# Index scores of two heads side by side, four buffers of positive parts, four selection rounds of the first tile made early and one of the longest tile made late

## The chip, the cores and the metric

One core of a Trainium2 chip. The metric is the device time of one execution in microseconds (us), lower is better. The kernel before takes 760.4 us (median of 3 runs, 760.36 to 760.41).

Engines are named as the profile names them: PE is TensorE (matrix products), DVE is VectorE, ACT is ScalarE, POOL is GpSimd, SP is SyncE (here the engine that issues most DMAs). PSUM has eight banks of 512 float32 columns.

## What is computed

One layer over 1024 frames of width 1024, batch 1. A projection of the normed input yields the operands of a differential attention (A, 4 heads) and of a sparse attention (B, 8 heads). For B an indexer with 4 heads of width 64 scores every key of every query; each query keeps its 256 best keys:

```
idx_logits = jnp.einsum('bqhd,bkd->bqhk', iqb, ik).astype(jnp.float32)
score = jnp.einsum('bqh,bqhk->bqk', iwb.astype(jnp.float32) * idx_scale,
                   jax.nn.relu(idx_logits))
score = jnp.where(allowed[None], score, -jnp.inf)
_, sel = lax.top_k(score, k_sel)
```

Both branches are gated, joined, projected out, added to x and normed. A frame sees keys up to the end of its own chunk of 64 frames.

## The kernel before

Everything is hand-ordered. Each engine has one instruction list, written out in its own function; engines wait for each other on counting semaphores. Queries go in eight tiles of 128 frames; tile i sees 128*(i+1) keys. Tiles 0 and 1 see at most 256 keys, so only tiles 2 to 7 (`SEL0` = 2) need a selection.

The work comes in this order on PE: turns of x; the indexer's projection in two halves of 512 frames (`project_idx`); the index scores (`score_idx`); the projections of A (`project`, 32 chunks of weights); the attention of A (`attend_all`); the projections of B; the attention of B (`attend_chosen`); the output projection.

**Index scores.** `score_idx(n)` is the product of head n % 4 for tile 2 + n // 4, so n runs from 0 to 23. Even heads lie in the partitions 0 to 63, odd heads in 64 to 127. Each column piece of a score is two matmul records in the trace, since the operands are float32. Scores 0 to 5 are spread over the second half of `project_idx`, one between two blocks of it, since they need only the first half of the keys; the first eight use the banks 1 and 2 in turn, and the later ones four pairs of banks, so that score n waits until the positive part of n-4 (of n-2 for the first eight) has been taken. ACT takes the positive part (`relu_of(n)`) from PSUM into one of two buffers:

```
if n >= 2:
    act.wait_ge(idx_added, n - 1)
act.activation(relu[:, n % 2, 0:length], idx_scores(n, 0, length), ACT.Relu
```

DVE multiplies it by the head's weight and adds it to the tile's score (`add_idx(n)`, L1569 for a tile's first head, L1572 for the others). Around these, ACT and DVE split the turned input for PE into a high and a low part (`high_h`, L788; `low_h`, L1474), and DVE moves the index weights (`move_iwT`, L1546; `move_iw`) and the second half of the keys (`ikT`, L1594), which score 8 is the first to need. The first projection of A starts when the positive part of score 20 has been taken (`idx_relu` 21), and its third, fifth and seventh bank when those of 21, 22 and 23 have.

**Selection.** `select(rounds, first, end)` takes per round and tile the 8 greatest scores (MAX8, L1624) and replaces them by the value `TAKEN` (MATCH_REPLACE8, L1629, with a short MATCH_VALUE_LOAD in front). 256 keys are 32 rounds (for tile 2, which sees 384 keys, the 128 worst are taken off in 16 rounds on the negated scores). All of this is DVE's. 16 rounds of tiles 2 to 7 and one of tiles 6 and 7 lie ahead of the attention of A, the rest of tiles 3 to 7 behind it, during the projections of B. ACT makes a mask of each finished tile (`make_masks`, in `CHOSEN_ORDER`), then moves the last projection of B into `mixB`, which lies on the memory of the scores, and POOL adds masks to bias bands (`near`, L740). The attention of B begins with tile 5 and comes to tile 7 as its seventh.

Of the kernel before, what the change touches and what calls it, by code (L numbers as in the profile page):

```python
# [21 lines left out]
SEQ, D_MODEL = 1024, 1024  # L22
P = 128
# [26 lines left out]
BAND = 2 * P  # L50
SW = 3


# [21 lines left out]
def build(nc, x, norm_w, w_in, w_out, lambda_q1, lambda_k1, lambda_q2, lambda_k2, subln_w,  # L75
# [79 lines left out]
    iwT, _ = place("iwT", [IDX_HEADS, SEQ], f32, at=mask_at)  # L155
    relu, _ = place("relu", [P, 2, SEQ], f32, at=probs_at)
    table, _ = place("table", [BUCKETS, A_HEADS + B_HEADS], f32, at=probs_at)
# [35 lines left out]
    with ctx:  # L193
        def sem(name):
            return ctx.enter_context(nc.semaphore(name))
# [54 lines left out]
        idx_added = sem("idx_added")  # L250
        mask_made = sem("mask_made")
        chosen = sem("chosen")
        mask_bias_made = sem("mask_bias_made")
# [174 lines left out]

        CHOSEN_ORDER = (SEL0, TILES - 2, TILES - 1, *range(SEL0 + 1, TILES - 2))

# [145 lines left out]
        def _(pool):  # L576
# [156 lines left out]
            def near(k):  # L733

                s, m = divmod(near_units[k], 2)
                b, i = place_of(1, s)
                if k >= NEAR:
                    pool.wait_ge(max_ready, 2 * STEPS + near_units[k - NEAR] + 1)
                end = score_off[i] + P * (i + 1)
                pool.tensor_tensor(near_slot(k), bias[:, A_HEADS + 2 * b + m, :], mask[:, end - BAND:end], ALU.add  # L740
                                   ).then_inc(near_made, 1)

            pool.wait_ge(mask_made, TILES - SEL0)
            ahead = [0]
# [27 lines left out]
        def _(act):  # L772
# [64 lines left out]
            def move(g):  # L837
                kind = GROUPS[g][2]
                for t in range(4 if g == Q_GROUP else 0, 8):
# [10 lines left out]
                    else:  # L850
                        if g == B_GROUPS[3] and t == 0:
                            act.wait_ge(mask_made, TILES - SEL0)
                        ins = act.activation((mixA if g == A_GROUPS[3] else mixB)[:, t, :], bank(t),
# [55 lines left out]
            def relu_of(n):  # L909

                length = P * (SEL0 + n // IDX_HEADS + 1)
                act.wait_ge(idx_ready, n + 1)
                if n >= 2:
                    act.wait_ge(idx_added, n - 1)
                act.activation(relu[:, n % 2, 0:length], idx_scores(n, 0, length), ACT.Relu
                               ).then_inc(idx_relu, 1)
# [7 lines left out]
            for n in range(3):  # L924
                relu_of(n)
                high_h(DB + 5 + n)
            high(DB)
            relu_of(3)
            high(DB + 1)
            relu_of(4)  # L930
            high(DB + 2)
            relu_of(5)
            move_iq(1, 0)
# [121 lines left out]
        def _(pe):  # L1055
# [211 lines left out]
            for n in range(3):  # L1267
                score_idx(n)
                project_idx(1, n + 2)
                turn_late(n + 5)  # L1270
            for n in range(3, 6):
                score_idx(n)
                project_idx(1, n + 2)
            score_idx(6)
# [174 lines left out]
        def _(dve):  # L1449
# [109 lines left out]
            def add_idx(n):  # L1559
# [3 lines left out]
                dve.wait_ge(idx_relu, n + 1)  # L1563
                r = relu[:, n % 2, 0:P * (i + 1)]
                if i == SEL0:
# [9 lines left out]
                if h == IDX_HEADS - 1:  # L1575
                    dve.wait_ge(idx_added, n + 1)
                    hidden = score_off[i] if i == SEL0 else score_off[i] + P * (i + 1) - CHUNK
                    link(dve.memset(score[0:CHUNK, hidden:hidden + CHUNK], -UNSEEN if i == SEL0 else UNSEEN))

            move_iwT(0)  # L1580
            low_h(DB + 2)
# [5 lines left out]
            for n in range(3):  # L1587
                add_idx(n)
                low_h(DB + 5 + n)
            for n in range(3, 6):  # L1590
                add_idx(n)
            move_iwT(1)
# [24 lines left out]
            dve.memset(mask_bias[:, 1:2], -MASK_BIAS / 2).then_inc(mask_bias_made, 1)  # L1617

            def select(rounds, first=SEL0, end=TILES, done=()):

                for k in range(rounds):
                    for i in range(first, end):
                        sc = score[:, score_off[i]:score_off[i] + P * (i + 1)]
                        ins = dve.max(top8[:, i - SEL0, :], sc)  # L1624
                        if i == end - 1:
                            link(ins)
                    for i in range(first, end):
                        sc = score[:, score_off[i]:score_off[i] + P * (i + 1)]
                        ins = dve.match_replace(sc, top8[:, i - SEL0, :], sc, TAKEN)  # L1629
                        if k == rounds - 1 and i in done:  # L1630
                            ins.then_inc(chosen, 1)
                        elif i == end - 1:
                            link(ins)

# [92 lines left out]

            select(FIRST, done=(SEL0,))
            select(1, TILES - 2)
            far_min(0, 0, 0)  # L1730
# [21 lines left out]
            link(dve.memset(bias[0:CHUNK, A_HEADS:nh, BAND - CHUNK:BAND], MASKED))  # L1752
            select(ROUNDS - FIRST - 3, SEL0 + 1, done=(TILES - 2, TILES - 1))
            dve.wait_ge(chosen, 3)
            select(1, SEL0 + 1, TILES - 2, done=range(SEL0 + 1, TILES - 2))
            def finishB(s):

# [22 lines left out]

            dve.wait_ge(mask_made, TILES - SEL0)
            far_min(1, 0, 0)
# [85 lines left out]
```

## Time and profile before

| | |
|---|---|
| median of 3 runs | 760.4 us |
| the profiled execution | 760.52 us, of which the span of its instructions 758.6 us |
| PE | 745.5 us busy, 98% |
| DVE | 596.0 us busy, 79% |
| POOL | 348.4 us busy, 46% |
| ACT | 326.3 us busy, 43% |
| granted TensorE clock | 0.999 of full |

The span is the time between the first and the last instruction in the trace; 1.9 us of the execution lie around it. A busy share is an average over stages; the trace has to be read by stage. A row of the timeline has start, length, engine, line, operation, output<-inputs, shape and count; what stands in brackets is how long the engine had been idle before it and who ended that.

### The profile page before, as it was taken

How to read it: one execution, taken by the hardware profiler on the slowest of the kernel's cores; microseconds unless marked ns; L12 is line 12 of the kernel's file. 1: busy time of each engine (PE TensorE's matmuls, PEld its weight loads, DVE VectorE, ACT ScalarE, POOL GpSimd, SP SyncE). 2: the span in 40 equal slices, each digit the busy share in tenths (PEclk: the TensorE clock that was granted, in tenths of full speed). 3: DMA queues.
4: the chain of work that ended last, by engine and by line, in shares of the span. 5: the costliest groups of instructions: out<-in, count | busy, mean ns of one | idle time of the engine just before them, and what ended most of it. 6: DMA issues, size and time to landing. Idle time of an engine off the chain costs nothing.

```text
span 758.6 us, 11943 instructions
## 1 busy us (share of the span) xinstructions
PE 745.5 (98%) x4184; PEld 635.3 (84%) x4184; DVE 596.0 (79%) x1269; ACT 326.3 (43%) x731; POOL 348.4 (46%) x429
## 2 busy tenths in 40 slices
PE   8999999999999999999999999999999999999996
PEld 7756888888888898899888888888999999988886
DVE  5548999999999989888699999996756667435444
ACT  7447122131314666667521221327666666423222
POOL 5220222223556868761334555639999994300000
PEclk9999999999999999999999999999999999999999
DMA  7341111111220010012021111220012022213131
GB/s 275 102 113 54 41 52 47 47 50 46 71 65 1 1 42 20 24 49 79 17 69 55 45 54 43 56 56 28 16 43 57 1 72 71 98 56 106 61 111 57
DMA packets 24564, 44.58 MB, mean 59 GB/s; under 512 B 3076, under 2 KB 10936, under 8 KB 24376
## 3 DMA queue, kind: packets, MB, share of 16 engines
q1 hardware_dynamic: 23352, 42.76, 18.9%
q10 hardware_dynamic: 1152, 1.05, 0.4%
q8 instruction: 34, 0.56, 0.3%
q14 instruction: 26, 0.21, 0.1%
HBM read 35.40 MB, written 6.57 MB: 55 GB/s over the span
## 4 chain that ended last, share of the span: by engine, by line
PE 92%; DVE 3%; issue 2%; ACT 1%; POOL 1%; POOLq 0%; ACTq 0%; DVEq 0%
PE psum L1245 40%; PE psum L1346 12%; PE psum L1443 12%; PE psum L1328 6%; PE psum L1306 4%; PE psum L1309 4%; PE psum L1165 3%; PE psum L1200 3%; PE psum L1137 3%; PE psum L1183 2%; PE psum L1313 1%; PE psum L1361 1%; PE psum L1312 1%; PE psum L1059 1%; DVE probs L1711 1%
## 5 line engine op out<-in xcount | busy, mean ns | idle before, releaser
L597 POOL TENSOR_TENSOR w_lo<-w_raw,w_hi 128x512 fp32r<-128x512 f32 x60 | 77.8, 1299 | 220.0 <-ACT w_hi L781 219.6
L1629 DVE MATCH_REPLACE8 score<-top,score 128x768 f32<-128x768 f32 (+5 forms) x176 | 157.3, 906 | 0.0
L1624 DVE MAX8 top<-score 128x8 f32<-128x768 f32 (+5 forms) x176 | 148.2, 909 | 1.0
L781 ACT ACTIVATE w_hi<-w_raw 128x512 fp32r<-128x512 f32 x60 | 37.6, 630 | 211.9 <-PE psum L1245 208.9
L957 ACT ACTIVATE probs<-psum,small 128x384 f32<-128x384 f32 (+7 forms) x128 | 94.7, 741 | 41.9 <-DVE small L1650 29.8
L1245 PE MATMUL psum<-w_hi,big_hi 128*128 128x512 f32 x256 | 99.6, 389 | 0.0
L1245 PE MATMUL psum<-w_lo,big_hi 128*128 128x512 f32 x256 | 99.6, 389 | 0.0
L1245 PE MATMUL psum<-w_hi,big_lo 128*128 128x512 f32 x256 | 99.6, 389 | 0.0
L1245 PE MATMUL psum<-big_hi,w_hi 128*128 128x512 f32 x192 | 74.8, 390 | 0.0
L1245 PE MATMUL psum<-big_hi,w_lo 128*128 128x512 f32 x192 | 74.7, 389 | 0.0
L1245 PE MATMUL psum<-big_lo,w_hi 128*128 128x512 f32 x192 | 74.7, 389 | 0.0
L1346 PE MATMUL psum<-v,probsT_B 128*128 128x64 f32 x576 | 70.3, 272 | 0.0
L1346 PEld LDWEIGHTS psum<-v,probsT_B 128*128 128x128 f32 x576 | 68.7, 192 | 1.1 <-DVE mixB L1764 0.2
L1328 PE MATMUL psum<-ident,probs 128*128 128x128 f32 x432 | 63.5, 274 | 0.5 <-ACT probsT_B L968 0.3
L1245 PEld LDWEIGHTS psum<-w_hi,big_lo 128*128 128x128 f32 x256 | 48.0, 188 | 10.1
L1245 PEld LDWEIGHTS psum<-w_lo,big_hi 128*128 128x128 f32 x256 | 48.0, 188 | 9.9
L1245 PEld LDWEIGHTS psum<-w_hi,big_hi 128*128 128x128 f32 x256 | 48.0, 188 | 9.9
L1650 DVE TENSOR_REDUCE small<-psum 128x1 f32<-128x384 f32 (+7 forms) x64 | 48.0, 751 | 8.3 <-PE psum L1313 7.5
L1443 PE MATMUL psum<-big_hi,mx_hi 128*128 128x512 f32 (+1 forms) x136 | 51.9, 381 | 0.0
L1328 PEld LDWEIGHTS psum<-ident,probs 128*128 128x128 f32 x432 | 50.3, 147 | 1.6 <-issue 0.5
L1443 PE MATMUL psum<-big_hi,mx_lo 128*128 128x512 f32 (+1 forms) x136 | 51.3, 377 | 0.0
L1443 PE MATMUL psum<-big_lo,mx_hi 128*128 128x512 f32 (+1 forms) x136 | 51.2, 377 | 0.0
(190 smaller groups left out, 1593.8 us busy)
## 6 DMA issues: line engine op xcount, KB each, us to landing
w_raw<-in_w_in SPq DMA_DIRECT2D x62, 256.0 KB, 2.7
xs<-in_x SPq DMA_DIRECT2D x8, 512.0 KB, 7.0
k_high_twice<-k_high_twice SPq DMA_DIRECT2D x16, 256.0 KB, 3.8
xres<-in_x SPq DMA_DIRECT2D x8, 512.0 KB, 4.1
out_y<-y_out SPq DMA_DIRECT2D x8, 384.0 KB, 3.0
w_tail<-in_w_out SPq DMA_DIRECT2D x10, 256.0 KB, 2.9
bias_scratch<-bias_row SPq DMA_DIRECT2D x1, 2304.0 KB
bias<-bias_scratch SPq DMA_DIRECT2D x12, 128.0 KB, 3.1
```

What stands on the lines that cost most here:

```text
L597: pool.tensor_tensor(lo[:, 0:cols], w_staged(n)[:, 0:cols], hi[:, 0:cols].bitcast(f32), ALU.subtract).then_inc(w_lo_made, 1)
L781: act.activation(w_parts(n)[0][:, 0:cols], w_staged(n)[:, 0:cols], ACT.Copy).then_inc(w_hi_made, 1)
L957: act.activation(probs_of(ph, s, m)[:, 0:length], score_of(u, 0, length), ACT.Exp, bias=negmax[:, u % 4:u % 4 + 1], scale=-1.0, accum_out= ...
L1245: ins = pe.matmul(o, a, b, start=(d == 0 and k == 0), stop=(d == DB - 1 and k == 2))
L1306: pe.matmul(o, q[:, qt], k[:, c:c + w], start=True, stop=False)
L1309: ins = pe.matmul(o, q[:, qt], low[:, c:c + w], start=False, stop=not banded)
L1328: ins = pe.transpose(bank(T_BANK + q % 2)[:, k * P:(k + 1) * P], p[:, (j + k) * P:(j + k + 1) * P], ident[:, :])
L1346: ins = pe.matmul(o, probsT[ph][:, q % 4, k * P:(k + 1) * P], v[:, j + k, cols], start=(j + k == 0), stop=(j + k == i))
L1443: ins = pe.matmul(o, a[:, t % 2, e, :], w[:, e, cols], start=(e == 0 and k == 0), stop=(e == DB - 1 and k == 2))
L1624: ins = dve.max(top8[:, i - SEL0, :], sc)
L1629: ins = dve.match_replace(sc, top8[:, i - SEL0, :], sc, TAKEN)
L1650: dve.tensor_reduce(negmax[:, u % 4:u % 4 + 1], score_of(u, 0, P * (i + 1)), AX.X, ALU.min).then_inc(max_ready, 1)
```

## The change

It has four parts.

1. In the second half of the index projection, PE makes the scores of two heads in direct succession (0 and 1, 2 and 3, 4 and 5) behind blocks 2, 3 and 4 of the projection; blocks 5, 6 and 7 follow with no score between them. ACT and DVE follow the same order.
2. The positive parts have four buffers (`RELUS` = 4), so `relu_of(n)` waits for the sum of n-4 where it waited for that of n-2.
3. Four of the sixteen rounds of tile 2 are made as soon as its score is summed (`FIRST_EARLY` = 4), between `low_h` of the last block and the move of the index weights and keys.
4. The one round of tile 7 that lay ahead of the attention of A is made behind all others, at the end of the selection; the mask of tile 7 is made by DVE itself, with a semaphore of its own (`last_mask_made`), for which POOL, ACT and DVE wait only where they need tile 7 or the memory of its score.

```diff
-        CHOSEN_ORDER = (SEL0, TILES - 2, TILES - 1, *range(SEL0 + 1, TILES - 2))
+        CHOSEN_ORDER = (SEL0, TILES - 2, *range(SEL0 + 1, TILES - 2))
...
                         if g == B_GROUPS[3] and t == 0:
-                            act.wait_ge(mask_made, TILES - SEL0)
+                            act.wait_ge(mask_made, len(CHOSEN_ORDER))
+                        if g == B_GROUPS[3] and t == TILES - 2:
+                            act.wait_ge(last_mask_made, 1)
...
-                if n >= 2:
-                    act.wait_ge(idx_added, n - 1)
-                act.activation(relu[:, n % 2, 0:length], idx_scores(n, 0, length), ACT.Relu
+                if n >= RELUS:
+                    act.wait_ge(idx_added, n - RELUS + 1)
+                act.activation(relu[:, n % RELUS, 0:length], idx_scores(n, 0, length), ACT.Relu
...
             for n in range(3):
-                score_idx(n)
+                score_idx(2 * n)
+                score_idx(2 * n + 1)
                 project_idx(1, n + 2)
                 turn_late(n + 5)
-            for n in range(3, 6):
-                score_idx(n)
-                project_idx(1, n + 2)
+            for d in range(5, DB):
+                project_idx(1, d)
...
             for n in range(3):
-                add_idx(n)
+                add_idx(2 * n)
+                add_idx(2 * n + 1)
                 low_h(DB + 5 + n)
-            for n in range(3, 6):
-                add_idx(n)
+            select(FIRST_EARLY, SEL0, SEL0 + 1)
             move_iwT(1)
...
-            select(FIRST, done=(SEL0,))
-            select(1, TILES - 2)
+            select(FIRST - FIRST_EARLY, done=(SEL0,))
+            select(FIRST_EARLY, SEL0 + 1)
+            select(1, TILES - 2, TILES - 1)
...
-            select(ROUNDS - FIRST - 3, SEL0 + 1, done=(TILES - 2, TILES - 1))
-            dve.wait_ge(chosen, 3)
+            select(ROUNDS - FIRST - 3, SEL0 + 1, done=(TILES - 2,))
+            dve.wait_ge(chosen, 2)
             select(1, SEL0 + 1, TILES - 2, done=range(SEL0 + 1, TILES - 2))
+            select(1, TILES - 1)
+            last_score = score[:, score_off[TILES - 1]:score_off[TILES - 1] + SEQ]
+            dve.tensor_scalar(mask[:, score_off[TILES - 1]:score_off[TILES - 1] + SEQ], last_score, TAKEN, MASKED,
+                              ALU.not_equal, ALU.mult).then_inc(last_mask_made, 1)
```

DVE's list from the split of the fifth block of the second half to the move of the keys, before (line 1474 is `low_h`, 1569 and 1572 are `add_idx`, 1546 is `move_iwT`, 1594 the copy of the keys):

```order
L1474 SCALAR_TENSOR_TENSOR big_lo<-psum,nw,big_hi 128x512
L1569 TENSOR_SCALAR score<-relu,iw 128x384
L1474 SCALAR_TENSOR_TENSOR big_lo<-psum,nw,big_hi 128x512
L1572 SCALAR_TENSOR_TENSOR score<-relu,iw,score 128x384
L1578 MEMSET score 64x64
L1569 TENSOR_SCALAR score<-relu,iw 128x512
L1572 SCALAR_TENSOR_TENSOR score<-relu,iw,score 128x512
L1546 TENSOR_SCALAR iwT<-psum 4x512
L1594 COPY ikT<-psum 64x512 x2
```

The same place in the changed kernel, from the sum of score 2 on (line 1478 is `low_h`, 1573 and 1576 `add_idx`, 1589 and 1594 a round of the selection, 1550 and 1614 the moves; of the four early rounds one is shown, and three more like it follow it):

```order
L1576 SCALAR_TENSOR_TENSOR score<-relu,iw,score 128x384 x2
L1582 MEMSET score 64x64
L1478 SCALAR_TENSOR_TENSOR big_lo<-psum,nw,big_hi 128x512
L1573 TENSOR_SCALAR score<-relu,iw 128x512
L1576 SCALAR_TENSOR_TENSOR score<-relu,iw,score 128x512
L1478 SCALAR_TENSOR_TENSOR big_lo<-psum,nw,big_hi 128x512
L1589 MAX top_71<-score 128x8
L1594 MATCH_REPLACE score<-top_71,score 128x384
...
L1550 TENSOR_SCALAR iwT<-psum 4x512
L1614 COPY ikT<-psum 64x512 x2
```

The sums now lie ahead of the last split, and the rounds stand where the sums of scores 3 to 5 stood, ahead of the move of weights and keys.

The end of the selection on DVE in the changed kernel (line 1763 makes the mask of tile 7; the row before the first one here is the last round of tiles 3 to 7; ISA at 1659 is the first step of the attention of B, `far_min`, which before followed directly on the row with 128x768):

```order
L1589 MAX top_71<-score 128x8 x3
L1594 MATCH_REPLACE score<-top_71,score 128x512
L1594 MATCH_REPLACE score<-top_71,score 128x640
L1594 MATCH_REPLACE score<-top_71,score 128x768
L1589 MAX top_71<-score 128x8
L1594 MATCH_REPLACE score<-top_71,score 128x1024
L1763 TENSOR_SCALAR mask<-score 128x1024
L1659 ISA psum,small<-psum,mask 128x512
```

A round of tile 7 and one more instruction now lie between the last round of tiles 3 to 5 and the attention of B.

## Rows read from the trace of the kernel before

**Rows 1.** The page, its first part: busy time, share, instructions.

```profile
PE 745.5 (98%) x4184; PEld 635.3 (84%) x4184; DVE 596.0 (79%) x1269; ACT 326.3 (43%) x731; POOL 348.4 (46%) x429
```

**Rows 2.** Busy us by stretch: length, PE, PEld, DVE, ACT, POOL; granted clock; DMA.

```profile
34.20:54.40 20.20, 20.20 (x79) 12.04 (x78) 7.79 (x12) 7.95 (x14) 4.12 (x3) 1.00 0.44 118
54.40:71.60 17.20, 16.65 (x73) 9.12 (x72) 14.73 (x22) 12.58 (x18) 0.00 (x0) 1.00 0.25 76
71.60:246.70 175.10, 175.10 (x775) 145.11 (x775) 172.25 (x309) 43.77 (x71) 61.92 (x55) 1.00 0.16 46
```

**Rows 3.** PE's timeline from 34 to 72 us, around the index scores (L1165).

```profile
34.20 0.91 PE L1165 MATMUL psum<-ikT,iqT 64*128 64x384 f32 x2
35.03 0.45 PE L1137 MATMUL psum<-big_hi,widx_hi 128*68 128x512 f32 x1
...
47.84 1.12 PE L1165 MATMUL psum<-ikT,iqT 64*128 64x512 f32 x2
48.89 0.45 PE L1137 MATMUL psum<-big_hi,widx_hi 128*68 128x512 f32 x1
...
54.41 1.13 PE L1165 MATMUL psum<-ikT,iqT 64*128 64x512 f32 x4
...
56.23 1.83 PE L1165 MATMUL psum<-ikT,iqT 64*128 64x512 f32 x8 [0.34 <-ACT relu L915]
...
71.63 0.50 PE L1245 MATMUL psum<-big_hi,w_hi 128*128 128x512 f32 x1
```

**Rows 4.** ACT's timeline: positive parts of scores 6 and 7, and of 19.

```profile
55.58 1.08 ACT L915 ACTIVATE relu<-psum 128x512 f32<-128x512 f32 x2 [0.46 <-PE psum L1165]
...
68.75 0.92 ACT L915 ACTIVATE relu<-psum 128x896 f32<-128x896 f32 x1 [0.37 <-DVE score L1572]
```

**Rows 5.** DVE's timeline from 45 to 71 us.

```profile
45.59 0.75 DVE L1474 SCALAR_TENSOR_TENSOR big_lo<-psum,nw,big_hi 128x512 fp32r<-128x512 f32 x1 [2.24 <-ACT big_hi L788]
46.49 1.38 DVE L1572 SCALAR_TENSOR_TENSOR score<-relu,iw,score 128x384 f32<-128x384 f32 x1
...
53.70 0.68 DVE L1546 TENSOR_SCALAR iwT<-psum 4x512 f32<-4x512 f32 x1
54.42 1.40 DVE L1594 COPY ikT<-psum 64x512 f32<-64x512 f32 x2
...
63.19 3.26 DVE L1572 SCALAR_TENSOR_TENSOR score<-relu,iw,score 128x768 f32<-128x768 f32 x3
...
67.50 3.66 DVE L1572 SCALAR_TENSOR_TENSOR score<-relu,iw,score 128x896 f32<-128x896 f32 x3
```

**Rows 6.** POOL's timeline at the end of the index projection.

```profile
46.16 2.83 POOL L597 TENSOR_TENSOR w_lo<-w_raw,w_hi 128x512 fp32r<-128x512 f32 x2 [21.60 <-ACT w_hi L781]
```

**Rows 7.** Groups of DVE by shape, the selection: busy us, mean ns of one.

```profile
L1624 DVE MAX8 top<-score 128x8 f32<-128x1024 f32 x32 | 38.7, 1209 | 0.0
...
L1629 DVE MATCH_VALUE_LOAD score<-top,score 128x8 f32 x176 | 14.6, 83 | 1.1
...
L1624 DVE MAX8 top<-score 128x8 f32<-128x384 f32 x16 | 9.0, 560 | 0.5
L1629 DVE MATCH_REPLACE8 score<-top,score 128x384 f32<-128x384 f32 x16 | 8.7, 543 | 0.0
```

**Rows 8.** DVE's timeline where the attention of A begins.

```profile
246.70 1.07 DVE L1650 TENSOR_REDUCE small<-psum 128x1 f32<-128x384 f32 x2 [0.72 <-PE psum L1313]
```

**Rows 9.** Timelines before B's attention (DVE, ACT, POOL), and a 1024-wide TENSOR_SCALAR.

```profile
526.18 0.70 DVE L1655 CUSTOM_DVE_ANT_0 psum<-psum,mask 128x512 f32<-128x512 f32 x1 [5.98 <-PE psum L1309]
...
521.26 4.69 ACT L853 ACTIVATE mixB<-psum 128x512 f32<-128x512 f32 x8
...
527.55 0.90 ACT L957 ACTIVATE probs<-psum,small 128x768 f32<-128x768 f32 x1 [0.30 <-DVE small L1678]
...
521.32 2.57 POOL L740 TENSOR_TENSOR near_low<-bias,mask 128x256 f32<-128x256 f32 x4 [0.50 <-ACT mask L874]
...
71.38 0.75 DVE L1569 TENSOR_SCALAR score<-relu,iw 128x1024 f32<-128x1024 f32 x1
```

More of the change, by code:

```diff
@@ L51 @@
 SW = 3
+RELUS = 4
+FIRST_EARLY = 4
 def bucket_selector():
@@ L155, in build @@
     iwT, _ = place("iwT", [IDX_HEADS, SEQ], f32, at=mask_at)
-    relu, _ = place("relu", [P, 2, SEQ], f32, at=probs_at)
+    relu, _ = place("relu", [P, RELUS, SEQ], f32, at=probs_at)
     table, _ = place("table", [BUCKETS, A_HEADS + B_HEADS], f32, at=probs_at)
@@ L251, in build @@
         mask_made = sem("mask_made")
+        last_mask_made = sem("last_mask_made")
         chosen = sem("chosen")
@@ L736, in near @@
                 b, i = place_of(1, s)
+                if i == TILES - 1:
+                    pool.wait_ge(last_mask_made, 1)
                 if k >= NEAR:
@@ L741, in near @@
                                    ).then_inc(near_made, 1)
-            pool.wait_ge(mask_made, TILES - SEL0)
+            pool.wait_ge(mask_made, len(CHOSEN_ORDER))
             ahead = [0]
@@ L924, in _ @@
             for n in range(3):
-                relu_of(n)
+                relu_of(2 * n)
+                relu_of(2 * n + 1)
                 high_h(DB + 5 + n)
[L927 to L932, printed above, removed]
+            for n in range(DB, DB + SW):
+                high(n)
             move_iq(1, 0)
@@ L1563, in add_idx @@
                 dve.wait_ge(idx_relu, n + 1)
-                r = relu[:, n % 2, 0:P * (i + 1)]
+                r = relu[:, n % RELUS, 0:P * (i + 1)]
                 if i == SEL0:
@@ L1578, in add_idx, with select @@
                     link(dve.memset(score[0:CHUNK, hidden:hidden + CHUNK], -UNSEEN if i == SEL0 else UNSEEN))
+            def select(rounds, first=SEL0, end=TILES, done=()):
+                for k in range(rounds):
+                    for i in range(first, end):
+                        sc = score[:, score_off[i]:score_off[i] + P * (i + 1)]
+                        ins = dve.max(top8[:, i - SEL0, :], sc)
+                        if i == end - 1:
+                            link(ins)
+                    for i in range(first, end):
+                        sc = score[:, score_off[i]:score_off[i] + P * (i + 1)]
+                        ins = dve.match_replace(sc, top8[:, i - SEL0, :], sc, TAKEN)
+                        if k == rounds - 1 and i in done:
+                            ins.then_inc(chosen, 1)
+                        elif i == end - 1:
+                            link(ins)
             move_iwT(0)
@@ L1617, in _ @@
             dve.memset(mask_bias[:, 1:2], -MASK_BIAS / 2).then_inc(mask_bias_made, 1)
[L1619 to L1633, printed above, removed]
             def later(ins):
@@ L1779, in mix_low @@
                                       ).then_inc(mixT_lo, 1)
-            dve.wait_ge(mask_made, TILES - SEL0)
+            dve.wait_ge(mask_made, len(CHOSEN_ORDER))
+            dve.wait_ge(last_mask_made, 1)
             far_min(1, 0, 0)
```

## The prediction, made before the changed kernel ran

> **What bounds the kernel now.** I read the page first: PE is busy 745.5 of 758.6 us [rows 1], so work that PE stops doing, or waits that it stops making, are what can be won, and the other engines matter only where PE waits for them. Next I read busy time by stretch [rows 2]. While the second half of the index projection runs (34.2 to 54.4 us), PE is busy all of its 20.2 us, DVE 7.8 and ACT 8.0: PE is the bound and the others have room. From 54.4 to 71.6 us DVE is busy 14.7 of 17.2 us, ACT 12.6, while PE's weight loads take 9.1: this stretch is a chain between three engines. Then come 175 us of projections in which PE is busy all the time and so is DVE, with the selection. The granted clock is 1.00 in all of these (2.4 GHz), so no part of the sum hangs on the clock.
>
> Third, PE's timeline [rows 3]. One score alone, 384 keys wide, holds PE from 34.20 to 35.03 us; one of 512 keys from 47.84 to 48.89. At 54.41 scores 6 and 7 stand together: four matmul records in 1.13 us, where two records took 1.12. So a second head, on the other half of the partitions, costs nothing when it directly follows the first. This row is of the kernel before; only scores 0 to 5 stand apart there.
>
> Last, the two places where DVE's selection meets PE. At the start of the attention of A, DVE waited 0.72 us for PE [rows 8]: DVE was on time by less than a microsecond. At the start of the attention of B it waited 5.98 us [rows 9], so its selection ended at 520.20.
>
> **Part 1, the pairs.** PE loses three slots: those of scores 1 and 3 (384 wide, 35.03 - 34.20 = 0.83 each) and one of the 512-wide pair 4 and 5 (48.89 - 47.84 = 1.05) [rows 3]. That is 2.7 us. Three entries from the projection's full array into the half array go too; I can't read their price from one row, and take 0 to 0.3 us for them. Score 1 now waits earlier for the move of the band and the index weights on DVE; those precede the split whose wait on ACT leaves DVE over 2 us idle, and lie before 34.2 us. Nothing else on PE waits: the splits that blocks 5 to 7 need are done one block ahead, behind two positive parts and two sums instead of one, in a stretch where ACT and DVE are idle over half of the time [rows 2].
>
> The Trainium skill (TensorEngine Tiling (Array Packing), Key Properties) says that tiles operate independently but that a change of the tiling mode drains TensorE; by the first half three slots go, as the rows say, and by the second somewhat more than their length goes, which is the 0 to 0.3 us above.
>
> **Part 3, the early rounds, and what they put off.** They stand ahead of the move of the keys, which score 8 needs. The last split began at 45.59 us [rows 5]; in the new order it comes 0.2 us later (block 4 now follows a 512-wide pair, 1.05, and not a 384-wide score, 0.83), so DVE comes free at about 46.5. A round of 384 is 0.56 + 0.54 us and a value load of 0.08 [rows 7]; each of the two steps waits for the one before, and I add 0.03 to 0.04 us for each of these: 1.24 us, four make 5.0 us, to 51.5. Then the index weights and keys: 0.72 us to the start of the copies and 1.40 for them [rows 5] bring 53.6 us. Without the rounds score 8 would start where PE and ACT allow: at 56.23 before [rows 3], right behind the first positive part of the pair 6 and 7 (55.58 and some 0.6, half of 1.08 and an overlap [rows 4]), less 2.7 to 3.0, that is 53.2 to 53.5. The rounds thus hold score 8 back by 0.1 to 0.4 us, whatever part 1 gives above 2.6. I take **2.6 us** for parts 1 and 3 together at this point, 2.2 to 2.9 as bounds. The sums of 6 and 7 and all that follow move by the same.
>
> **Part 2, four buffers.** From 60 us on DVE sums without a gap, so DVE's own times don't move against score 8; what moves is who waits for it. Before, the positive part of score 19 waited for the sum of 17, the first of the three sums at 67.50 that make 3.66 us; with a step of 1.25 us it ends at 68.65, and the part starts at 68.75 (0.37 us idle, ended by DVE) and takes 0.92 [rows 4, 5]. Score 23 needs its bank, starts at 69.7 and ends in 1.8 to 1.9 us, and at 71.63 A's projections begin [rows 3]. With four buffers the same part waits for the sum of 15, the last of three that start at 63.19 and take 3.26: 66.45 us. That is 68.65 - 66.45 = **2.2 us** earlier, if ACT and PE are ready then. I stepped through them with the durations of the trace and the waits of the changed list, and it is close: ACT ends the part of 18 at about 66.5, and PE by itself, with pairs of 1.3 to 1.7 us, could be done by 68.5 against the 69.4 that this step asks for. So the three engines are nearly equal, and I keep 1.4 as the low bound and 2.3 as the high. The parts of 21, 22 and 23 end in time for the third, fifth and seventh bank: the last one waits for the sum of 19, at 67.50 + 3.66 = 71.16, and ends at 72.2, while PE, begun at 69.4, comes to the seventh bank 4.1 us later at 73.5.
>
> The Trainium skill (TensorEngine Tiling (Array Packing), PSUM Bottleneck) says that tiling speeds up TensorE but not the emptying of PSUM, which may then bind. By it the pairs could not pay where ACT and DVE bind; here they don't in the stretch of part 1, and part 2 acts on just that bound in the next.
>
> **At the attention of A.** PE comes 2.6 + 2.2 = 4.8 us earlier. DVE comes earlier by 2.6, by four rounds of tile 2 in the interleaved list (some 1.0 each, 4.0) and by a round of tile 7 (about 2.3, from 1.21 for each step [rows 7] less overlap): 8.9 us. Its 0.72 us of waiting [rows 8] becomes 4.8. Without parts 3 and 4 it would be 2.6 + 0.72 = 3.3 against 4.8, and PE would wait 1.5 us: that is what the moved rounds bring, and the cover that the sum needs.
>
> **At the attention of B, part 4.** All is shifted by 4.8 us; I keep the old times. After 520.20 us DVE makes one round of 1024: 1.21 + 0.08 + 1.21 [rows 7] and the joints, 2.6. Then the mask of tile 7, which no row shows: at least 0.75 us (a TENSOR_SCALAR of the same width [rows 9]), at most the 1.21 of the other passes over 1024. I take 0.9, since it is nearest to the first. It ends at 523.7, 2.4 us before DVE's first work there (526.18). ACT reaches the bank that waits for it at 521.26 + 6 x 0.59 = 524.8 [rows 9], 1.1 us later still than the mask. POOL needs tile 7 much later. Price: nothing.
>
> **Sum.** 2.6 + 2.2 = 4.8 us. The profiled execution took 760.52 us, 1.9 around its span of 758.6, 0.1 from the median; its span becomes 753.8 and the median 760.4 - 4.8 = **755.6 us**. What follows each of the shifted points (attention, output projection) has the same order as before.
>
> **The rivals.**
>
> *The pairs alone (chance 0.10).* ACT or PE bind in the index scores, and the four buffers bring less than 1 us. For it: the three engines are within a microsecond there. Against it: ACT was idle for DVE ahead of the part of 19, and the next bound, PE's, is 0.9 us away. Time 760.4 - 2.6 - 0.5 = 757.3.
>
> *The mask of tile 7 comes late (0.06).* The seven bands that POOL makes from 521.32 us on (0.64 each, to 525.8 [rows 9]) would stretch or stop DVE's mask step. For it: at 46.49 a sum of 384 took 1.38 us beside POOL's work at 46.16 [rows 5, 6], where sums of 768 take 1.09. If the mask waited for the last band, it would be made at 526.6; ACT's last two banks would end at 527.8 and not 525.95, and the first exponential, at 527.55 with 0.30 us to spare, would come 1.5 us late: 755.6 + 1.5 = 757.1. Against it: by the 768-wide sums a 384-wide one takes at most 0.7 us, so POOL cost that sum 0.7 to 0.8; put here, these leave the mask before 524.8. The Trainium skill (GPSIMD Engine Reference, Specifications table) says that GpSimd's interfaces to SBUF are shared with VectorE and contended for by instructions with two SBUF inputs or in a two-port mode; the sum above is of the first kind and the trace agrees, and the mask step could be of the second.
>
> *Slower (0.03).* The early rounds hold the keys back for much longer than 5 us. For a loss of 1.5 us they would have to put score 8 off by some 6.5 us more, a round of 2.8 us and not 1.24. It is decided at 2.4 us a round (no change). Against it: 16 such rounds are in the trace, at 0.56 and 0.54. Time about 762.
>
> *No change (0.03).* PE wins its 4.8 us and waits for them at one of the two attentions. It takes a DVE that is 9 us later at A, or 7 at B, than worked out above.
>
> **How the numbers follow.** The forecast has 0.78; its own range is 2.2 + 1.4 = 3.6 to 2.9 + 2.3 = 5.2 us won, 755.2 to 756.8. The range reaches on to the first two rivals and a little to the fast side, for startup waits that I hold fixed: 754.7 to 757.4. What can be told from no change is 0.2%, 1.5 us: faster 0.94, same 0.03, slower 0.03.
>
> **What would show it.** In the changed profile: four records of scores at each of about 34.2, 37.7 and 41.3 us, in no more time than two took; scores 6 and 7 at 51.4 to 51.7; score 8 at 53.6, behind the copy of the keys; the part of 19 no longer idle for more than 0.1 us for DVE; the first projection of A at 66.8; DVE idle 4 to 5 us at the start of A's attention near 242, and 2 to 3 us at B's. It would be wrong if the first projection came after 68, or PE had a new wait of a microsecond at either attention.

## The result, and the profile after

The changed kernel takes 755.55 us (median of 4 runs, 754.80 to 757.23) against 760.40 us; the ratio is 0.9939, with a 95% interval of 0.9926 to 0.9951. (Here and below the ratio is taken over all executions, so it is not exactly that of the two medians.) A second set of runs of the changed kernel took 755.68 us (5 runs, 754.96 to 757.45). The profiled execution took 755.46 us, its span is 753.7 us, where 753.8 was forecast.

Busy time in the stretches that answer to [rows 2], of the changed kernel (us, then PE, PEld, DVE, ACT, POOL, granted clock, DMA):

```profile
34.20:51.40 17.20, 17.20 (x80) 11.45 (x80) 11.20 (x24) 7.89 (x15) 3.81 (x3) 1.00 0.48 139
51.40:66.80 15.40, 13.80 (x73) 8.48 (x70) 13.52 (x20) 12.25 (x17) 0.00 (x0) 1.00 0.29 85
66.80:241.90 175.10, 175.10 (x775) 145.18 (x776) 167.91 (x297) 43.45 (x71) 61.96 (x56) 1.00 0.17 46
```

The first stretch is 3.0 us shorter and the second 1.8; the third is as long as before, and DVE has 7 us free in it where it had 3.

PE's timeline of the changed kernel, answering to [rows 3]; L1169 is `score_idx`, L1249 the first projection of A:

```profile
34.00 0.92 PE L1169 MATMUL psum<-ikT,iqT 64*128 64x384 f32 x4
37.53 0.92 PE L1169 MATMUL psum<-ikT,iqT 64*128 64x384 f32 x4
41.06 1.13 PE L1169 MATMUL psum<-ikT,iqT 64*128 64x512 f32 x4
...
51.06 1.13 PE L1169 MATMUL psum<-ikT,iqT 64*128 64x512 f32 x4
...
53.54 1.36 PE L1169 MATMUL psum<-ikT,iqT 64*128 64x512 f32 x8 [1.02 <-DVE ikT L1614]
55.48 11.24 PE L1169 MATMUL psum<-ikT,iqT 64*128 64x512 f32 x56 [0.58 <-DVE iw L1560]
66.66 0.50 PE L1249 MATMUL psum<-big_hi,w_hi 128*128 128x512 f32 x1
```

Three pairs of four records each take 0.92, 0.92 and 1.13 us, where two records took 0.91 and 1.12. There are two waits with a new owner: 1.02 us for the keys in front of score 8 and 0.58 for the index weights in front of score 10. What lies ahead of score 0 does not take the same time in every trace: score 0 starts at 33.64 to 34.37 us, in one trace at 35.40. So times in this stage are best counted from score 0, which starts at 34.20 before and at 34.00 after. The first projection then starts 37.43 us behind it before and 32.66 after: 4.77 us are won. The span is 4.9 us shorter; the 0.20 us by which score 0 itself starts earlier more than cover the rest.

DVE's timeline of the changed kernel (L1478 `low_h`; L1589 and L1594 a round of selection; L1550 and L1614 the moves; L1576 the sums; L1654 and L1659 the first steps of A and of B; L1763 the mask of tile 7), answering to [rows 5, 8, 9]:

```profile
45.62 0.75 DVE L1478 SCALAR_TENSOR_TENSOR big_lo<-psum,nw,big_hi 128x512 fp32r<-128x512 f32 x1 [1.42 <-ACT big_hi L793]
46.29 0.55 DVE L1589 MAX8 top<-score 128x8 f32<-128x384 f32 x1
46.87 0.09 DVE L1594 MATCH_VALUE_LOAD score<-top,score 128x8 f32 x1
46.95 0.54 DVE L1594 MATCH_REPLACE8 score<-top,score 128x384 f32<-128x384 f32 x1
47.53 0.56 DVE L1589 MAX8 top<-score 128x8 f32<-128x384 f32 x1
...
51.28 0.69 DVE L1550 TENSOR_SCALAR iwT<-psum 4x512 f32<-4x512 f32 x1
52.00 1.40 DVE L1614 COPY ikT<-psum 64x512 f32<-64x512 f32 x2
...
60.42 3.26 DVE L1576 SCALAR_TENSOR_TENSOR score<-relu,iw,score 128x768 f32<-128x768 f32 x3
...
241.73 1.07 DVE L1654 TENSOR_REDUCE small<-psum 128x1 f32<-128x384 f32 x2 [4.93 <-PE psum L1317]
...
517.69 1.12 DVE L1763 TENSOR_SCALAR mask<-score 128x1024 bf16<-128x1024 f32 x1
521.22 0.70 DVE L1659 CUSTOM_DVE_ANT_0 psum<-psum,mask 128x512 f32<-128x512 f32 x1 [2.41 <-PE psum L1313]
```

A round takes 47.53 - 46.29 = 1.24 us. At A's attention DVE now waits 4.93 us for PE and at B's 2.41.

ACT's timeline of the changed kernel, the positive parts of scores 19 and 20 and the moves in front of B's attention, answering to [rows 4, 9]:

```profile
63.77 1.93 ACT L922 ACTIVATE relu<-psum 128x896 f32<-128x896 f32 x2 [0.20 <-DVE score L1576]
...
516.26 4.70 ACT L860 ACTIVATE mixB<-psum 128x512 f32<-128x512 f32 x8
...
522.60 0.90 ACT L961 ACTIVATE probs<-psum,small 128x768 f32<-128x768 f32 x1 [0.34 <-DVE small L1682]
```

The part of 19 starts 0.09 us after the sum of 15 (60.42 + 3.26 = 63.68). The eight moves take 4.70 us (4.69 before), so the one that waits for the mask of tile 7 is not held.

### The profile page after: what moved, and what is told of

Read it like the earlier page. It is cut to its first block, busy times and chain, and to the rows that moved or that the text cites. A ratio compares the mean times of both kernels' runs of the same rounds, so it can differ in the third digit from the quotient of the medians.

```text
span 753.7 us, 11948 instructions
## 1 busy us (share of the span) xinstructions
PE 740.0 (98%) x4184; PEld 634.4 (84%) x4184; DVE 597.6 (79%) x1270; ACT 324.4 (43%) x730; POOL 348.2 (46%) x429
## 3 DMA queue, kind: packets, MB, share of 16 engines
q1 hardware_dynamic: 23352, 42.76, 19.4%
q10 hardware_dynamic: 1152, 1.05, 0.4%
HBM read 35.40 MB, written 6.57 MB: 56 GB/s over the span
## 4 chain that ended last, share of the span: by engine, by line
PE 91%; DVE 4%; issue 2%; ACT 1%; POOL 1%; DVEq 0%; POOLq 0%; ACTq 0%
PE psum L1249 40%; PE psum L1350 12%; PE psum L1447 12%; PE psum L1332 6%; PE psum L1310 4%; PE psum L1313 4%; PE psum L1204 3%; PE psum L1187 2%; PE psum L1169 2%; PE psum L1141 2%; PE psum L1317 1%; PE psum L1365 1%; PE psum L1316 1%; PE psum L1063 1%; DVE probs L1715 1%
## 5 line engine op out<-in xcount | busy, mean ns | idle before, releaser
L1594 DVE MATCH_REPLACE8 score<-top,score 128x640 f32<-128x640 f32 (+5 forms) x176 | 157.4, 906 | 0.0
L1589 DVE MAX8 top<-score 128x8 f32<-128x640 f32 (+5 forms) x176 | 148.7, 910 | 1.1
L1249 PE MATMUL psum<-w_hi,big_hi 128*128 128x512 f32 x256 | 99.6, 389 | 0.0
L1249 PE MATMUL psum<-w_lo,big_hi 128*128 128x512 f32 x256 | 99.6, 389 | 0.0
L1249 PE MATMUL psum<-w_hi,big_lo 128*128 128x512 f32 x256 | 99.6, 389 | 0.0
L1249 PE MATMUL psum<-big_hi,w_hi 128*128 128x512 f32 x192 | 74.8, 390 | 0.0
L1249 PE MATMUL psum<-big_hi,w_lo 128*128 128x512 f32 x192 | 74.7, 389 | 0.0
L1249 PE MATMUL psum<-big_lo,w_hi 128*128 128x512 f32 x192 | 74.7, 389 | 0.0
L1654 DVE TENSOR_REDUCE small<-psum 128x1 f32<-128x384 f32 (+7 forms) x64 | 48.0, 752 | 12.5 <-PE psum L1317 11.7
L1249 PEld LDWEIGHTS psum<-w_lo,big_hi 128*128 128x128 f32 x256 | 48.1, 188 | 10.0
L1249 PEld LDWEIGHTS psum<-w_hi,big_lo 128*128 128x128 f32 x256 | 48.1, 188 | 10.0
L1249 PEld LDWEIGHTS psum<-w_hi,big_hi 128*128 128x128 f32 x256 | 48.1, 188 | 9.8
```

Of the source, the lines that this page charges most:

```text
L1249: ins = pe.matmul(o, a, b, start=(d == 0 and k == 0), stop=(d == DB - 1 and k == 2))
L1654: dve.tensor_reduce(negmax[:, u % 4:u % 4 + 1], score_of(u, 0, P * (i + 1)), AX.X, ALU.min).then_inc(max_ready, 1)
```

## The experiments

Each time below was measured beside the kernel before on the same chip: 760.45 us (12 runs) for the first four, 760.39 (20) for the next four, 760.24 (9) for the last four. "Behind score 0" is the start of the first projection of A counted from the start of score 0, from each run's trace; before it is 37.43 us, after 32.66.

### The pairs alone

The kernel before, with the loops of part 1 on PE, ACT and DVE, and nothing else:

```diff
             for n in range(3):
-                score_idx(n)
+                score_idx(2 * n)
+                score_idx(2 * n + 1)
                 project_idx(1, n + 2)
                 turn_late(n + 5)
-            for n in range(3, 6):
-                score_idx(n)
-                project_idx(1, n + 2)
+            for d in range(5, DB):
+                project_idx(1, d)
```

> The kernel before with part 1 alone: the six early scores in pairs, two buffers, the selection as before. Theory (three score slots leave PE, and nothing else moves): the first projection of A begins 2.7 to 3.0 us earlier than before, DVE reaches the attention of A as much earlier, keeps its 0.7 us of waiting there, and the time falls by 2.7 to 3.0 us, to 757.4 to 757.7. Rival (the gain of the whole change is made by the buffers and the pairs only move work): less than 1 us, above 759.4.

Measured: 757.26 us (757.12 to 757.75, 5 runs), ratio 0.9961 (0.9949 to 0.9974); 34.27 us behind score 0, so 3.16 us won there, just above the 2.7 to 3.0 us expected. DVE waits 0.73 us at the attention of A, as before. The slots themselves are worth 2.7 us; the 0.45 above them stands at the borders between projection and score. PE's timeline, one line of the kernel before, then two of the changed kernel (L1141 is `project_idx`):

```profile
51.13 1.12 PE L1165 MATMUL psum<-ikT,iqT 64*128 64x512 f32 x2
```

```profile
46.78 0.39 PE L1141 MATMUL psum<-big_hi,widx_hi 128*68 128x512 f32 x1
...
48.87 0.39 PE L1141 MATMUL psum<-big_hi,widx_hi 128*68 128x512 f32 x1
```

Before, the block of the projection between scores 4 and 5 lasts from 48.89 [rows 3] to 51.13, 2.24 us; in the changed kernel block 6, with a block on either side, lasts from 46.78 to 48.87, 2.09. So a block that stands between two scores takes 0.15 us more, and three of the seven places where PE goes from the projection into a score are gone. What PE does at the border these rows don't show.

### The buffers alone

The kernel before, with four buffers (`RELUS` = 4), on DVE's side too:

```diff
-    relu, _ = place("relu", [P, 2, SEQ], f32, at=probs_at)
+    relu, _ = place("relu", [P, RELUS, SEQ], f32, at=probs_at)
...
-                if n >= 2:
-                    act.wait_ge(idx_added, n - 1)
+                if n >= RELUS:
+                    act.wait_ge(idx_added, n - RELUS + 1)
```

> The kernel before with part 2 alone: four buffers of positive parts, all orders as before. Theory (the buffers bring PE 2.2 us, but DVE's sums don't end earlier, so at the attention of A, where DVE had 0.72 us to spare, PE waits for the selection): the first projection of A begins 2.2 us earlier (at 69.4 us), the attention of A only 0.7 us earlier, the time falls by 0.7 us to 759.7. Rival (the buffers' gain stands by itself and needs no moved rounds): a fall of 2.2 us, to 758.2.

Measured: 758.48 us (757.61 to 758.78, 8 runs), ratio 0.9974 (0.9963 to 0.9984); 35.23 us behind score 0. PE's timeline of this kernel, the scores from 10 on:

```profile
58.31 11.24 PE L1166 MATMUL psum<-ikT,iqT 64*128 64x512 f32 x56 [0.20 <-DVE iw L1557]
```

The same 56 records took 13.44 us before: 2.20 us, as worked out. But the time fell by 2.0 us and not by 0.7: the rival holds. DVE was late at the attention of A, as foreseen; its timeline and ACT's in this kernel (L1651 is A's first step on DVE, L958 the table load and the exponentials):

```profile
245.95 1.75 DVE L1651 TENSOR_REDUCE small<-psum 128x1 f32<-128x384 f32 x3
...
244.52 1.28 ACT L958 ACT_TABLE_LOAD   x1
246.54 0.58 ACT L958 ACTIVATE probs<-psum,small 128x384 f32<-128x384 f32 x1 [0.74 <-DVE small L1651]
```

DVE's first step, which stands 0.86 us behind the first score of A when it is in time (240.87 and 241.73 in the changed kernel), came 2.25 us behind it (243.70), so 1.39 us late. ACT loads its table until 245.80 in any case, so the first exponential was only 0.74 us late. The first three steps of DVE then ran without a gap, where it had waited 0.52 us for PE between the second and the third. From the first score of A to the first projection of B it took 126.12 us, against 126.05 before: a lateness of 1.39 us cost no more than 0.07, and the next experiment shows that even this can't be put down to it.

### Pairs and buffers, no round moved

The kernel before, with both edits above.

> The kernel before with parts 1 and 2, no round of the selection moved. Theory: the first projection of A begins 4.9 to 5.2 us earlier, DVE comes 2.7 to 3.0 us earlier and has 0.7 to spare, so PE waits about 1.5 us for it at the attention of A, and the time falls by 3.4 to 3.7 us, to 756.7 to 757.0. Rival (the moved rounds bring nothing, the whole gain is made in the index scores): a fall of 4.9 us, to 755.5.

Measured: 755.03 us (754.48 to 755.61, 5 runs), ratio 0.9931 (0.9919 to 0.9944); 32.07 us behind score 0, and 37.43 - 3.16 - 2.20 = 32.07 exactly. DVE's first step at A came 2.26 us behind the first score, 1.40 late, and A's attention took 126.29 us, 0.24 more than before. But these 0.24 us are not the price of the lateness. PE's timeline at A, the changed kernel first, then this one (L1310 and L1304 are a score of A, L1187 one of the products that stand between; the first score of A starts at 240.87 and 240.66):

```profile
244.27 0.50 PE L1310 MATMUL psum<-k_high_twice,q_low_high 128*128 128x512 f32 x1 [0.24 <-ACT probs L961]
...
246.82 0.48 PE L1187 MATMUL psum<-big_hi,wf_hi 128*128 128x512 f32 x1
...
248.06 0.50 PE L1310 MATMUL psum<-k_high_twice,q_low_high 128*128 128x512 f32 x1 [0.31 <-ACT probs L961]
...
253.12 0.50 PE L1310 MATMUL psum<-k_high_twice,q_low_high 128*128 128x512 f32 x1 [0.66 <-ACT probs L961]
```

```profile
244.80 0.50 PE L1304 MATMUL psum<-k_high_twice,q_low_high 128*128 128x512 f32 x1 [0.98 <-ACT probs L955]
...
248.12 0.40 PE L1304 MATMUL psum<-k_high_twice,q_low_high 128*128 128x512 f32 x1
...
252.92 0.51 PE L1304 MATMUL psum<-k_high_twice,q_low_high 128*128 128x512 f32 x1 [0.52 <-ACT probs L955]
```

Counted from the first score of A, these three stand at 3.40, 7.19 and 12.25 us in the changed kernel and at 4.14, 7.46 and 12.26 here: PE is 0.74 us late, then 0.27, then 0.01. It waits for exponentials at all three places even when DVE is in time, and the lateness goes into those waits; with the buffers alone the third stands at 12.27. The 0.2 us that the attention takes more come from a wait of 0.17 us some 70 us behind the first score (310.90), and the second trace of the changed kernel, where DVE is in time, has the same wait (0.16 us) and an attention of 126.20 us. So 5.4 us are won in the index scores, the median falls by 5.42, and nothing measurable is given back at A. The theory fell again: the moved rounds bring nothing that can be measured.

### The early rounds undone

The changed kernel with part 3 taken back; the late round of tile 7 stays:

```diff
-            select(FIRST_EARLY, SEL0, SEL0 + 1)
             move_iwT(1)
...
-            select(FIRST - FIRST_EARLY, done=(SEL0,))
-            select(FIRST_EARLY, SEL0 + 1)
+            select(FIRST, done=(SEL0,))
```

> The changed kernel with part 3 undone: the sixteen rounds of tile 2 stand together again ahead of the attention of A; pairs, buffers and the late round of tile 7 stay. Theory (the early rounds hold score 8 back by 0.3 to 0.4 us, and the late round of tile 7 alone is enough to keep DVE ahead of PE at the attention of A, by about 0.8 us): score 8 begins at 53.1 to 53.2 us and not at 53.54, the first projection 0.3 to 0.4 us earlier, and the time is 755.1 to 755.3, equal to the changed kernel or a little below. Rival (the early rounds carry part of the gain): 1 us or more above the changed kernel.

Measured: 755.26 us (754.93 to 755.63, 5 runs), ratio 0.9934 (0.9921 to 0.9946); 32.06 us behind score 0. PE's timeline of this kernel:

```profile
53.10 1.83 PE L1169 MATMUL psum<-ikT,iqT 64*128 64x512 f32 x8 [0.34 <-ACT relu L922]
55.13 11.24 PE L1169 MATMUL psum<-ikT,iqT 64*128 64x512 f32 x56 [0.20 <-DVE iw L1560]
```

Score 8 waits for ACT again, as before the change, and not for the keys. The early rounds cost 0.60 us of the first projection, where 0.3 to 0.4 were expected, and win nothing. DVE had 0.96 us to spare at A, where it was 1.40 late with pairs and buffers alone; the late round of tile 7 (part 4) is all that differs between these two kernels, and 755.26 and 755.03 us can't be told apart.

### Three early rounds, and eight

```diff
-FIRST_EARLY = 4
+FIRST_EARLY = 3
```

> The changed kernel with three early rounds of tile 2 and not four. Theory (the fourth early round is what holds the keys for score 8 back, by 0.6 us as the run without early rounds showed, and a round is 1.25 us): score 8 starts where PE and ACT allow, the first projection 0.6 us earlier than in the changed kernel, time lower by 0.4 to 0.6 us. Rival (what the run without early rounds won at score 8 came from elsewhere): no difference.

Measured: 755.12 us (754.82 to 755.23, 5 runs), ratio 0.9929 (0.9917 to 0.9942); 32.07 us behind score 0, the same as with no early round, as expected. The fourth alone makes the loss.

With `FIRST_EARLY = 8`:

> The changed kernel with eight early rounds of tile 2. Theory (from the fourth round on each early round puts off the keys, score 8 and everything behind it by 1.25 us): the first projection 5.0 us later than in the changed kernel, time 760.4 to 760.6, that is no gain left over the kernel before. Rival (the late keys are hidden again by the buffers or by DVE's earlier arrival at the attention of A): less than 2 us slower than the changed kernel.

Measured: 761.70 us (761.35 to 763.72, 9 runs), ratio 1.0020 (1.0011 to 1.0030): slower than the kernel before. Behind score 0 it is 39.49 us, 6.83 more than in the changed kernel, and only 5.0 of these are the four rounds: score 8 starts 24.53 us behind score 0 and not 19.54. PE's timeline, and busy time by stretch (columns as above) of this kernel:

```profile
58.40 0.59 PE L1118 MATMUL psum<-ident,iwT 4*128 4x4 f32 x4 [4.83 <-DVE iwT L1550]
59.93 15.04 PE L1169 MATMUL psum<-ikT,iqT 64*128 64x512 f32 x64 [0.94 <-DVE ikT L1614]
```

```profile
54.00:56.00 2.00, 0.00 (x0) 0.00 (x0) 1.90 (x6) 0.69 (x2) 0.00 (x0) 0.95 0.97 237
56.00:60.00 4.00, 0.66 (x6) 0.60 (x6) 3.80 (x8) 0.00 (x0) 0.00 (x0) 0.50 0.55 195
60.00:66.00 6.00, 6.00 (x20) 3.67 (x22) 3.74 (x7) 2.60 (x4) 0.00 (x0) 0.50 0.00 0
66.00:70.00 4.00, 4.00 (x25) 3.06 (x23) 3.39 (x6) 3.33 (x5) 0.00 (x0) 0.99 0.00 0
```

While PE stood idle for 4.83 us the granted clock fell from 1.00 to 0.50 (2.4 to 1.2 GHz), and it came back at about 66 us. From score 8 to the first projection it took 14.96 us where the changed kernel takes 13.12: the other 1.8 us, which are put down to the clock. The profiled execution is the slowest of the nine (763.72 us, the next 762.28), 1.2 us of it ahead of score 0. By the medians this kernel is 6.0 to 6.2 us behind the changed one, so in a typical execution some 1.0 to 1.2 us stand beside the 5.0 of the rounds.

### Three buffers

`RELUS = 3` in the changed kernel.

> The changed kernel with three buffers of positive parts. Theory (the positive part of score 19 waits for the sum of 16 and not for that of 15; between the two lie 0.9 us): the first projection 0.9 us later than in the changed kernel, time 756.3 to 756.5. Rival (PE or ACT bind with four buffers already, so that the third buffer gives nearly all): within 0.3 us of the changed kernel.

Measured: 756.62 us (756.53 to 756.72, 5 runs), ratio 0.9950 (0.9936 to 0.9963); 33.56 us behind score 0, 0.90 us more than with four. PE's timeline of this kernel:

```profile
55.71 12.15 PE L1169 MATMUL psum<-ikT,iqT 64*128 64x512 f32 x56 [0.58 <-DVE iw L1560]
```

13.44, 12.15 and 11.24 us for two, three and four buffers: each step is the distance between two sums on DVE (1.29 and 0.91).

### One more round ahead of the attention of A

The changed kernel, with a round of tiles 3 to 7 moved from behind A's attention to in front of it:

```diff
             select(1, TILES - 2, TILES - 1)
+            select(1, SEL0 + 1)
             far_min(0, 0, 0)
...
             finishA(STEPS - 1)
-            select(1, SEL0 + 1)
```

> The changed kernel with one more round of tiles 3 to 7 (9.2 us of DVE) ahead of the attention of A and one less behind it, so that DVE comes there 4.3 us late instead of 4.9 us early. Theory, formed from the runs with two buffers or pairs alone, where DVE was 1.4 to 1.5 us late and the attention of A took only 0.1 to 0.3 us more: ACT's table load and the first steps hide about the first 1.4 us, and the rest is paid, 2.6 to 3.0 us, time 758.1 to 758.6. Rival 1 (the attention of A takes up any lateness): within 0.5 us of the changed kernel. Rival 2 (my prediction's reading, each microsecond late is paid): 759.6 to 759.9.

Measured: 760.72 us (759.80 to 761.64, 11 runs), ratio 1.0004 (0.9995 to 1.0013); its profiled execution took 760.28. None of the three readings gives this. DVE's and PE's timelines in this kernel, then busy time by stretch (columns as above):

```profile
245.72 1.75 DVE L1654 TENSOR_REDUCE small<-psum 128x1 f32<-128x384 f32 x3
...
247.59 0.79 PE L1310 MATMUL psum<-k_high_twice,q_low_high 128*128 128x512 f32 x1 [3.92 <-ACT probs L961]
...
252.30 0.48 PE L1187 MATMUL psum<-big_hi,wf_hi 128*128 128x512 f32 x1
```

```profile
245.00:246.00 1.00, 0.00 (x0) 0.00 (x0) 0.96 (x2) 0.00 (x0) 0.92 (x2) 0.73 0.00 0
246.00:252.00 6.00, 4.41 (x15) 4.02 (x16) 4.67 (x7) 2.96 (x8) 4.22 (x5) 0.50 0.00 0
252.00:258.00 6.00, 6.00 (x37) 5.34 (x36) 5.33 (x10) 4.04 (x8) 1.90 (x4) 0.98 0.00 0
```

DVE's first step comes 5.21 us behind the first score of A (240.51) and not 0.86: 4.35 us late. PE's waits for exponentials in A's attention add up to 4.3 us where the changed kernel has 1.2, so 3.1 us of lateness came through and 1.3 were hidden, near what the theory has (2.6 to 3.0 paid). But the attention took 131.08 us, 5.0 more than the changed kernel's 126.03: the granted clock fell to 0.50 in PE's 3.9 us of idleness and stayed there to about 252 us. The remaining 1.9 us are its price: the same records, from the wait to the next L1187, took 4.71 us here (247.59 to 252.30) and 2.55 in the changed kernel (244.27 to 246.82). The split between wait and clock is not exact, since a slower PE also waits less afterwards. From one execution to the next the mean granted clock of this kernel was 0.993 to 0.997, and the four at 0.993 were the slowest (761.22 to 761.64 us, the others 759.80 to 760.94).

### The index weights first

In all three kernels that follow, DVE moves the second half of the index weights ahead of two sums:

```diff
+            move_iw(range(TILES // 2, TILES), bank(5), 2)
             for n in range(6, EARLY):
                 add_idx(n)
-            move_iw(range(TILES // 2, TILES), bank(5), 2)
```

They were run beside the changed kernel itself.

> The changed kernel once more, on the chip and in the hour of the next three, as their measure. Expected: 755.3 to 755.8 us, the first projection 32.7 us behind score 0.

Measured: 755.68 us (754.96 to 757.45, 5 runs), ratio 0.9946 (0.9933 to 0.9958); 32.65 us behind score 0.

> The changed kernel, but DVE moves the second half of the index weights ahead of the sums of 6 and 7 and not behind them. Score 10 waits for this move, and PE stood idle 0.6 us for it in the changed kernel's trace; DVE stood idle 0.3 and 0.35 us for positive parts behind it. Theory (DVE's sums set the pace from score 8 on, so the 0.65 us of its waiting are what can be won, less some 0.2 for the move, which loses its cover): the first projection 0.3 to 0.5 us earlier, time 755.0 to 755.3. Rival (the keys' late move has already set the pace): no difference.

Measured: 755.57 us (754.41 to 755.77, 5 runs), ratio 0.9934 (0.9920 to 0.9947); 32.39 us behind score 0, 0.26 less, a little under the 0.3 to 0.5 expected. The gain stands in the trace and is too small for the times.

> The same, with three early rounds and not four. Theory: the 0.6 us of the fourth round and 0.3 to 0.5 for the weights' move add up, time 754.4 to 754.8. Rival (both buy the same time): as with three early rounds alone, 755.1.

Measured: 754.87 us (754.56 to 755.13, 5 runs), ratio 0.9931 (0.9919 to 0.9944); 31.76 us behind score 0. DVE's and PE's timelines of this kernel:

```profile
52.44 0.17 DVE L1560 COPY iw<-psum 128x16 f32<-128x16 f32 x1 [0.41 <-PE psum L1118]
...
52.74 12.96 PE L1169 MATMUL psum<-ikT,iqT 64*128 64x512 f32 x64 [0.34 <-ACT relu L922]
65.63 0.50 PE L1249 MATMUL psum<-big_hi,w_hi 128*128 128x512 f32 x1
```

All scores from 8 on now run in one piece.

> The same move of the index weights, and no early rounds at all. Theory: score 8 starts at the same point as with three early rounds, DVE arrives at the attention of A with no more than 1 us in hand, time as with three early rounds within 0.2 us, 754.4 to 754.9.

Measured: 754.63 us (754.18 to 755.65, 5 runs), ratio 0.9931 (0.9918 to 0.9943); 31.75 us behind score 0. The two are 0.9 us ahead of the changed kernel in the trace, 0.8 and 1.05 us in the medians. The intervals of their ratios overlap that of the changed kernel beside them, so it is the traces that tell them apart.

## Why the prediction was right, and where not

The forecast was 755.6 us; the measured median is 755.55. That the two agree to 0.05 us is luck: the two medians of the changed kernel differ by 0.13, and single executions lie between 754.80 and 757.45.

**The pairs and the early rounds together: right in sum, wrong in the parts.** The text took 2.6 us for both at score 8. The pairs alone give 3.16, above the bound of 3.0: the three entries from the full array into the half one are worth 0.45 us and not 0 to 0.3. The signs to look for have the same error: scores 6 and 7 were to come at 51.4 to 51.7 us and came at 51.06. The early rounds cost 0.60 and not 0.1 to 0.4. Counted from score 0, score 8 starts at 18.86 without them, where 19.0 to 19.3 were forecast, and at 19.54 with them, where 19.4 was: each end is off by 0.14. The difference, 3.16 - 0.60 = 2.56, is what the text had, and this is not luck: it says that whatever the pairs give above 2.6 is lost again to the keys, and the runs with three early rounds and with none bear it out.

**The four buffers: right.** 2.20 us alone (2.2 forecast), the same beside the pairs, and 1.29 of these for the third buffer. The chain was the one named: a sum on DVE, the part of 19, score 23, the projection. One line on it was wrong: the part of 19 still waits 0.20 us for its sum. PE and ACT were ready in time, which the text called close, and DVE still sets the pace, which is why an earlier move of the index weights wins more.

**At the attention of A: the step that failed.** "Without parts 3 and 4 [...] PE would wait 1.5 us: that is what the moved rounds bring." DVE is indeed 1.4 us late without them, but PE is only 0.74 us late at the first place where it needs an exponential and 0.01 us late 12.3 us behind the first score of A. Shown in its place: ACT's table load, which ends at the same time in either case, hides the first half of the lateness; DVE catches up where it would have waited between its second and third step; and what is left goes into waits for exponentials (0.24, 0.31 and 0.66 us) that PE has there even when DVE is in time. The number was not part of the sum, so the sum came out; as a statement of what parts 3 and 4 are worth it is wrong. Together they lose a little: by the traces 0.59 us in the index scores, with nothing won at A; in the medians, which were not run side by side, pairs and buffers alone take 755.03 us and the whole change 755.55 and 755.68. A lateness of 4.35 us is no longer hidden, so the step was wrong in its size and in where it begins, not in its kind.

**At the attention of B: right.** The mask of tile 7 took 1.12 us (0.9 taken, 1.21 the bound), DVE waited 2.41 us behind it (2.4 forecast), and the first exponential came at the same distance as before. Beside the mask, POOL's first four bands took 3.03 us and not 2.57 (from 516.32), so the two did overlap, and POOL's bands took longer, with nobody waiting. Whether the mask step would be shorter away from POOL no run shows.

**The slower rival** named the right place and put the point of no gain a little too far off: at 2.4 us a round, or 4.8 us of delay. Four more rounds, 5.0 us, make the kernel slower than before by 1.3 us, since PE's idleness costs it clock as well. (Its 6.5 us for a loss of 1.5 should read 4.8 + 1.5 = 6.3.) *No change* asked for a DVE that is 9 us later at A; with one more round there it came 9.3 us later than in the changed kernel, and the time was that of the kernel before, of which 1.9 us again was clock. The fall of the clock was not in the prediction.

## What to carry to other kernels

Two half-height products on different halves of the array are worth placing side by side even if a third engine then has to take their results in bursts; what counts is whether that engine has idle time there, and each border between full and half array that goes is worth something by itself (0.15 us here). Where three engines pass buffers around, work out which event the last part waits for with one buffer more: the gain is the time between two such events (1.29 and 0.91 us for the third and the fourth buffer; a fifth was not tried). Work put into a gap is free only as long as the gap: the fourth round overran it by half a round, and the overrun was paid in full. An engine that comes late is paid for only where its lateness is longer than the waits that stand behind it anyway: 1.4 us were hidden here, 4.35 were not.

## What was not expected of the hardware

The granted clock went down to half after PE stood idle for 4.8 us in one run and 3.9 us in another, and stayed there for some 10 and 7 us, while in the kernels whose longest wait at these places was 1.0 us it stayed at 1.00. In these two traces that cost 1.8 and 1.9 us beyond the wait; by the medians of the first kernel it is nearer 1.0 to 1.2, so it varies from one execution to the next. The Trainium skill (TensorE: Matmul & The Clock Gate, Part 1: The HAM clock gate) describes such a gate, and these two traces agree that an idle PE loses clock; its two levels are the ones seen here.

A one-column step of DVE at the start of A's attention took 0.81 us in the changed kernel, beside a two-input step of POOL (243.97 to 245.25), and 0.22 us in the kernel with pairs and buffers alone, where it came as that step of POOL ended. This is 0.6 us of the 1.4 that the late DVE made up. Whether that meeting decides how much is hidden was not tried.
